# Prompt latent attention with the probabilities as the loaded operand of the values

## What is computed

```
s = (einsum("bqhn,bkhn->bhqk", qn, k_nope)
     + einsum("bqhe,bke->bhqk", qp, k_pe)) * (64 + 32) ** -0.5
mask = k_chunk[None, :] <= (pos // 64)[:, None]
p = softmax(where(mask, s, -inf), axis=-1)
return einsum("bhqk,bkhe->bqhe", p, v)      # v has 64 columns a head
```

## Time and profile before

| what | value |
|---|---|
| median of 3 runs | 3055.38 us (3051.51 to 3055.81) |
| profiled execution | 3043.57 us, span 3042.0 us |
| PE busy | 2723.2 us (90%), 17464 matmuls |
| weight loads (PEld) busy | 2505.8 us (82%) |
| DVE busy | 1467.0 us (48%) |
| ACT busy | 941.2 us (31%) |
| POOL busy | 252.0 us (8%) |
| mean granted TensorE clock | 0.939 of full speed |
| chain that ended last | PE 77%, DVE 6%, issue 6%, ACT 4% |

### The profile page before, as it was taken

How to read it: one execution, slowest core, us unless ns; L and a number is a source line. 1 busy time by engine, 2 the same in 40 slices (tenths; PEclk the granted TensorE clock), 3 DMA queues, 4 the chain that set the end, 5 groups by cost and what they waited for, 6 DMA issues and landing times.

```text
span 3042.0 us, 53054 instructions
## 1 busy us (share of the span) xinstructions
PE 2723.2 (90%) x17464; PEld 2505.8 (82%) x17464; DVE 1467.0 (48%) x2602; ACT 941.2 (31%) x2032; POOL 252.0 (8%) x684
## 2 busy tenths in 40 slices
PE   5898989789889899999988889997997999999996
PEld 5875879667689899999978568885776988999996
DVE  5635221244444674655657342213445347646375
ACT  3324223345421331322233332233453113323122
POOL 3100100110000010100001011011000001001010
PEclk8979989889999999999989899998999999999998
DMA  4220114411122222222123002234111222222222
GB/s 124 52 60 0 51 44 124 149 44 42 39 62 63 67 69 73 73 69 74 58 65 70 27 8 64 68 116 134 42 39 42 76 63 66 69 73 73 69 69 75
DMA packets 376797, 201.32 MB, mean 66 GB/s; under 512 B 66438, under 2 KB 368636, under 8 KB 376658
## 3 DMA queue, kind: packets, MB, share of 16 engines
q1 hardware_dynamic: 346722, 178.99, 21.0%
q10 hardware_dynamic: 25344, 12.27, 1.3%
q0 software_dynamic: 4592, 8.35, 0.9%
HBM read 183.84 MB, written 17.88 MB: 66 GB/s over the span
## 4 chain that ended last, share of the span: by engine, by line
PE 77%; DVE 6%; issue 6%; ACT 4%; DVEq 3%; DMA 2%; ACTq 1%; SPq 0%; POOL 0%; POOLq 0%
PE ps L547 21%; PE ps L551 20%; PE ps L548 20%; PE ps L687 1%; PE ps L644 1%; PE ps L714 1%; DVE rstd L1638 1%; DMA k_past<-in_cache_a_k 1%; ACT w_hi L1171 1%; PE ps L586 1%; PE ps L589 1%; PE ps L617 1%; PE ps L712 1%; DVEq L1749 1%; PE tp L702 1%
## 5 line engine op out<-in xcount | busy, mean ns | idle before, releaser
L547 PE MATMUL ps<-hn_hi,w_hi 128*128 128x328 f32 x2848 | 893.0, 320 | 13.7 <-DVE ob_lo L1937 7.7
L548 PE MATMUL ps<-hn_lo,w_hi 128*128 128x328 f32 x2848 | 878.3, 314 | 0.0
L551 PE MATMUL ps<-hn_hi,w_lo 128*128 128x328 f32 x2848 | 662.8, 315 | 0.0
L1620 DVE TENSOR_TENSOR w_lo<-w_raw,w_hi 128x1024 fp32r<-128x1024 f32 x300 | 366.9, 1223 | 511.4 <-ACT w_hi L1171 505.6
L1171 ACT ACTIVATE w_hi<-w_raw 128x1024 fp32r<-128x1024 f32 x300 | 316.7, 1057 | 849.0 <-PE ps L551 627.6
L547 PEld LDWEIGHTS ps<-hn_hi,w_hi 128*128 128x128 f32 x2848 | 539.1, 189 | 34.7 <-issue 29.8
L548 PEld LDWEIGHTS ps<-hn_lo,w_hi 128*128 128x128 f32 x2848 | 539.7, 190 | 0.2
L551 PEld LDWEIGHTS ps<-hn_hi,w_lo 128*128 128x128 f32 x2848 | 485.8, 189 | 0.0
L547 PE MATMUL ps<-s_hi,w_hi 128*128 128x328 f32 x704 | 220.7, 320 | 18.5 <-DVE w_lo L1620 14.0
L548 PE MATMUL ps<-s_lo,w_hi 128*128 128x328 f32 x704 | 220.3, 318 | 0.0
L551 PE MATMUL ps<-s_hi,w_lo 128*128 128x328 f32 x704 | 166.9, 320 | 0.0
(11 more groups left out here) (333 smaller groups left out, 4130.7 us busy)
## 6 DMA issues: line engine op xcount, KB each, us to landing
w_raw<-in_w_in SPq DMA_DIRECT2D x98, 512.0 KB
w_raw<-in_w_up SPq DMA_DIRECT2D x88, 512.0 KB
w_raw<-in_w_down SPq DMA_DIRECT2D x32, 512.0 KB
out<-tok_out ACTq DMA_DIRECT2D x32, 256.0 KB, 2.3
k_past<-in_cache_a_k SPq DMA_DIRECT2D x16, 512.0 KB, 5.0
v_past<-in_cache_a_v SPq DMA_DIRECT2D x16, 512.0 KB, 3.5
w_raw<-in_w_a_br SPq DMA_DIRECT2D x16, 512.0 KB
w_raw<-in_w_out SPq DMA_DIRECT2D x16, 512.0 KB
```

Of the source, the lines that this page charges most:

```text
L547: mm(dst[:, c, :], w_hi[:, slot, k, :], x_hi[:, k, cols], start=(k == 0), stop=False)
L548: mm(dst[:, c, :], w_hi[:, slot, k, :], x_lo[:, k, cols], start=False, stop=False)
L551: last = mm(dst[:, c, :], w_lo[:, slot, k, :], x_hi[:, k, cols], start=False, stop=(k == nk - 1))
L1620: tt(w_lo[:, slot], w_raw[:, slot], w_hi[:, slot].bitcast(F32), ALU.subtract).then_inc(w_split[slot], 1)
```

## The change

Four things are changed in `mla_prompt`; the rest of the kernel stays. `values` swaps its operands: the turned probabilities are loaded (128 columns) and the head's values move (64 columns), so that the output has the queries as rows. The probabilities are no longer divided: `finish` is gone, `turn` waits for "exp", and DVE's `outputs` multiplies the 128 x 64 output by the reciprocal sum while it copies it to a new buffer `o_tok` (128 queries x tile x 128, two heads side by side); the sums get four places. For each pair of heads and tile, PE turns `o_tok` once (`pair_tile`: in steps 6 and 7 of the pair and 0 and 1 of the next) into the free columns of `tq`, and DVE copies it to `obT`. The first pair is written out as well as the last, and at the end PE turns the last two tiles after a wait for all outputs, and DVE copies them.

```diff
--- before.py
+++ after.py
@@ -205,6 +205,7 @@
         d_e = (d_e0, d_e1)
         assert names["d_e0"][1] <= Z
         assert names["keyT"][0] >= names["tok_out"][1]
+        o_tok, = run(names["ckv_tok"][1], ("o_tok", [P, QT, P]))
 
         pdT2, = run(names["par_rows"][0], ("pdT2", [P, H, 2 * DEC]))
         o_sq, = run(names["par_rows"][0], ("o_sq", [P, 2, P]))
@@ -339,6 +340,10 @@
             first, last = (0, KD) if u // 2 % 2 == 0 else (0, 4)
             return [(last * (2 * (u % 2) + x) // 4, last * (2 * (u % 2) + x + 1) // 4) for x in range(2)]
 
+        def pair_tile(u, first):
+
+            return u - 6 if u >= 6 else (u + 2 if u < 2 and not first else None)
+
         OUTPUTS = STREAMS // 2 + 1
 
         block = ctx.enter_context(nc.Block())
@@ -621,7 +626,7 @@
                 def turn(i2, u):
                     i = u % QT
                     step = l * H * QT + i2 * 2 * QT + u
-                    e.wait_ge(a["p"], step + 1)
+                    e.wait_ge(a["exp"], step + 1)
                     e.wait_ge(a["pT"], step)
                     e.sem_inc(past_wait, 1)
                     p = ms[:, u % 2]
@@ -630,7 +635,7 @@
                         last = mm(tpt[0][:, 1 + k, :], p[:, META + P * k:META + P * (k + 1)], ident, is_transpose=True, start=True, stop=True)
                     last.then_inc(a["turned"], 1)
 
-                def values(i2, u):
+                def values(i2, u, first):
                     hh, i = divmod(u, QT)
                     step = l * H * QT + i2 * 2 * QT + u
                     if i == 0:
@@ -638,30 +643,39 @@
                     e.wait_ge(a["pT"], step + 1)
                     e.wait_ge(a["out_done"], step - 1 if u else step)
                     e.sem_inc(past_wait, 1)
-                    out = tq[VB * hh:VB * (hh + 1), u % 2, 0:P]
-                    mm(out, mla_vs[0:META, hh, 0, :], mla_eT[0:META, u % 2, 0, :], start=True, stop=False)
+                    tile = pair_tile(u, first)
+                    if tile is not None:
+                        mm(tq[:, u % 2, P:2 * P], o_tok[:, tile, :], ident, is_transpose=True, start=True, stop=True)
+                    out = tq[:, u % 2, 0:VB]
+                    mm(out, mla_eT[0:META, u % 2, 0, :], mla_vs[0:META, hh, 0, :], start=True, stop=False)
                     for k in range(i + 1):
-                        last = mm(out, mla_vs[:, hh, 1 + k, :], mla_eT[:, u % 2, 1 + k, :], start=False, stop=(k == i))
+                        last = mm(out, mla_eT[:, u % 2, 1 + k, :], mla_vs[:, hh, 1 + k, :], start=False, stop=(k == i))
                     last.then_inc(a["out"], 1)
 
-                def two_heads(i2, final):
+                def two_heads(i2, first, final):
                     for u in range(2 * QT):
                         then = step_after(i2, u, 2, final)
                         if then and u:
                             scores(*then)
                         if u:
-                            values(i2, u - 1)
+                            values(i2, u - 1, first)
                         turn(i2, u)
 
                     if not final:
                         scores(*step_after(i2, 2 * QT - 1, 3, final))
-                    values(i2, 2 * QT - 1)
+                    values(i2, 2 * QT - 1, first)
 
                 for u in range(3):
                     scores(0, u, first=u < 2)
-                with e.Fori(0, H // 2 - 1) as i2:
-                    two_heads(i2, False)
-                two_heads(H // 2 - 1, True)
+                two_heads(0, True, False)
+                with e.Fori(1, H // 2 - 1) as i2:
+                    two_heads(i2, False, False)
+                two_heads(H // 2 - 1, False, True)
+                e.wait_ge(a["out_done"], (l + 1) * H * QT)
+                e.sem_inc(past_wait, 1)
+                for i in range(2, QT):
+                    last = mm(tq[:, 0, (i - 1) * P:i * P], o_tok[:, i, :], ident, is_transpose=True, start=True, stop=True)
+                last.then_inc(a["p"], 1)
 
             def diff_prompt(l):
                 a = att["diff"]
@@ -1205,7 +1219,7 @@
                     e.wait_ge(a["max"], l * H * QT + i2 * 2 * QT + u + 1)
                     e.sem_inc(past_wait, 1)
                     c = 2 * (u % 2)
-                    act(ms[:, u % 2, 0:n], ms[:, u % 2, 0:n], ACT.Exp, bias=negmax[:, c:c + 1], accum_out=sums[:, c:c + 1]).then_inc(a["exp"], 1)
+                    act(ms[:, u % 2, 0:n], ms[:, u % 2, 0:n], ACT.Exp, bias=negmax[:, c:c + 1], accum_out=sums[:, u % 4:u % 4 + 1]).then_inc(a["exp"], 1)
 
                 def transposed(i2, u):
                     i = u % QT
@@ -1679,43 +1693,42 @@
                     e.drain()
                     ts(negmax[:, c:c + 1], maxes[:, c:c + 1], -1.0, None, ALU.mult).then_inc(a["max"], 1)
 
-                def finish(i2, u):
-                    n = META + P * (u % QT + 1)
-                    c = 2 * (u % 2)
-                    e.wait_ge(a["exp"], l * H * QT + i2 * 2 * QT + u + 1)
+                def outputs(i2, u, first):
+                    hh, i = divmod(u, QT)
+                    step = l * H * QT + i2 * 2 * QT + u
+                    c = u % 4
+                    e.wait_ge(a["exp"], step + 1)
                     e.sem_inc(past_wait, 1)
                     e.reciprocal(recips[:, c:c + 1], sums[:, c:c + 1])
                     e.drain()
-                    ts(ms[:, u % 2, 0:n], ms[:, u % 2, 0:n], recips[:, c:c + 1], None, ALU.mult).then_inc(a["p"], 1)
-
-                def outputs(i2, u):
-                    hh, i = divmod(u, QT)
-                    e.wait_ge(a["out"], l * H * QT + i2 * 2 * QT + u + 1)
-                    e.sem_inc(past_wait, 1)
-                    rows = slice(VB * hh, VB * (hh + 1))
-                    copy(one(obT[rows, ds(i2, 1), i * P:(i + 1) * P]), tq[rows, u % 2, 0:P]).then_inc(a["out_done"], 1)
-
-                def two_heads(i2, final):
+                    e.wait_ge(a["out"], step + 1)
+                    e.sem_inc(past_wait, 1)
+                    tile = pair_tile(u, first)
+                    if tile is not None:
+                        copy(one(obT[:, ds(i2 if u >= 6 else i2 - 1, 1), tile * P:(tile + 1) * P]), tq[:, u % 2, P:2 * P])
+                    ts(o_tok[:, i, VB * hh:VB * (hh + 1)], tq[:, u % 2, 0:VB], recips[:, c:c + 1], None, ALU.mult).then_inc(a["out_done"], 1)
+
+                def two_heads(i2, first, final):
                     for u in range(2 * QT):
-                        then = step_after(i2, u, 1, final)
-                        if then:
-                            finish(*then)
                         if u:
-                            outputs(i2, u - 1)
+                            outputs(i2, u - 1, first)
                         then = step_after(i2, u, 2, final)
                         if then:
                             maxima(*then)
                         e.drain()
-                    outputs(i2, 2 * QT - 1)
+                    outputs(i2, 2 * QT - 1, first)
 
                 for u in range(2):
                     maxima(0, u, first=True)
                 e.drain()
-                finish(0, 0)
+                two_heads(0, True, False)
+                with e.Fori(1, H // 2 - 1) as i2:
+                    two_heads(i2, False, False)
+                two_heads(H // 2 - 1, False, True)
+                e.wait_ge(a["p"], l + 1)
+                e.sem_inc(past_wait, 1)
+                copy(obT[:, H // 2 - 1, 2 * P:], tq[:, 0, P:3 * P])
                 e.drain()
-                with e.Fori(0, H // 2 - 1) as i2:
-                    two_heads(i2, False)
-                two_heads(H // 2 - 1, True)
 
             def diff_prompt(l):
                 a = att["diff"]
```

## The result

The changed kernel takes 3112.76 us (median of 4 runs, 3106.52 to 3121.66) against 3055.48 us before: 1.0195 times as long, 95% interval 1.017 to 1.022. It is slower by some 57 us; the forecast was 3105 us, 50 slower, for the reason that TensorE's clock would not come back. The profiled execution took 3106.52 us.

What follows compares the result with a forecast made beforehand. Bound: a VectorE and ScalarE chain at full clock, PE at half clock. Two stages of 122.5 us, 245 against 196.1, gave +49 us; on the median of 3055.4 that made 3105 us, range 3048 to 3130.

Steps and rivals of the forecast that it cites:

- two blocks of eight: A block is four steps (one head, tiles 0 to 3), eight a stage; two at full clock were assumed, 122.5 us a stage.
- Rival A: In the stages, the clock stays as now or better and the kernel is faster: 3048 us, 3029 at full clock throughout; chance 0.17.
- Rival B: In the values, narrow records are short (near 0.118 us), slow blocks take 14.0 us: +4 us, 3059 in all; chance 0.10.
- The block at 1.2 GHz: Four steps of one head at half clock, set by PE: 16.1 us against 15.8 before, bounds 14.0 and 18.0.
- The added turns: PE's two extra turns a block for the head pairs: 0.43 us at 1.2 GHz, 0.22 at 2.4 GHz.
- The meta product's wider load: In the values at half clock, this load is partly exposed: 0.06 us a tile, 0.24 a block.
- the time to the first values: The start of each stage, before the first values: 7 us, taken from the kernel before.
- The block at 2.4 GHz: Four steps of one head at full clock, set by PE's round trip through ScalarE: 9.84 us against 10.62, gaining 0.78.
- gaps: PE's waits between turn and values in a full-clock block, behind tile 0 filled by the widest scores: 4.27 us.
- values and meta products: PE's value records (20 x 0.117 = 2.34 us) and four meta pairs (1.44 us) in a full-clock block: 3.78 us.
- The tail: The stage's end, PE waiting for the last output, two turns, VectorE's copies: 0.8 us, between 0.3 and 1.5.

Runs made afterwards that it cites:

- absorb_after: The changed kernel, with the query absorption ahead of the stage moving 128 columns in its second product instead of 16; 3109.53 us, 1.0204 times the kernel before.
- wide: The changed kernel, with every value product moving its 64 columns twice (128 columns, second half unused); 3054.28 us, 1.0001 times the kernel before.
- fill: The changed kernel plus one unused PE product (128 rows, 256 columns moved) a step before the wait for ScalarE's copy; 3056.08 us, 1.0015 times before.
- fill_rows16: The changed kernel plus one unused PE product a step, 256 columns moved on 16 rows instead of 128; 3172.43 us, 1.0381 times the kernel before.

## Why the prediction was right

The sign, the cause and the size came out: +57 us measured, +50 forecast, within the range of 3048 to 3130. Point by point:

**The clock.** Forecast: the stages begin at 1.2 GHz as now and stay there mostly, with two blocks of eight at 2.4 GHz in each. Shown: none in layer 0 and some 2.7 in layer 1, so 2.7 in all and not 4. The number two was a choice and not worked out, and that the sum came so near is partly luck: in absorb_after, the same stage had 37.5 us at full clock in layer 0 and 2.4 in layer 1. That the narrower stream in the values is the cause is shown by wide (clock back, 58 us less, nothing else changed); the pair fill and fill_rows16 shows that idleness is not. Rival A, that less idleness keeps the clock, is out: its price of 3048 us needed as many blocks at full clock as before. The Trainium skill's page "TensorE: Matmul & The Clock Gate", section "The HAM clock gate", ties the clock to how busy PE is; here PE at 127.44 of 133.3 us busy got 0.50, and in fill_rows16 it lost the full clock after 17.10 of 17.10 us busy, so the measurements decide against that wording for products of this kind.

**The records.** Forecast 0.22 us apart at 1.2 GHz and about 0.117 at 2.4; measured 0.221 and 0.1175. Rival B (0.118 at the low clock, blocks of 14.0 us) is out. The same page of the Trainium skill, section "LDWEIGHTS (loading the stationary operand)", gives one formula for the load, by which 128 columns take 107 ns, and no clock with it. At 1.2 GHz the trace of after disagrees with it as rows 9 did, 0.221 us; at 2.4 GHz the measured 0.1175 us is near the page's figure.

**The block at 1.2 GHz.** Forecast 16.1 us; measured (15.96 + 16.46) / 2 = 16.2. That is nearer than its terms deserve. The added turns were put at 0.43 a block; against the first block, which has none (15.55), they cost 0.66. The meta product's wider load was put at 0.24 a block and costs nothing: the product takes 222.00 - 221.38 = 0.62 us, as it did in the kernel before (219.54 to 220.16). The two misses cancel. The whole stage at half clock was put at 135; layer 0 took 133.3, of which the time to the first values is 6.1 us (215.3 to 221.38) where 7 were taken over from before. So the first pair written out, which the forecast put at nothing, shows no cost there.

**The block at 2.4 GHz.** Forecast 9.84, measured 10.07, so a block gains 0.55 and not 0.78. The step that failed is one term of the sum, "The added turns of pairs: two a block, 0.22". By the lines 1766.00 and 1766.23 above, one such turn (L648) holds PE for 0.23 us, not the 0.112 of a turn in a row of turns: two take 0.46, and the missing 0.24 is that. The other terms hold (block from 1761.74): turns 1.52 against 1.57, gaps (1.00, 0.96, 1.08, 1.18) 4.22 against 4.27, values and meta products 3.84 against 3.78. As only 2.7 blocks ran so, it moved the result by under 1 us. These turns need no waited-for probabilities, yet stand behind the wait for them in PE's program, so that they come on top of the gap instead of filling it; to place them before that wait was not tried.

**The sum.** Forecast 245 us for both stages, measured 249.9. 1.3 blocks fewer at full clock cost some 8 us (6.1 each), and the shorter starts give back 1.8. The 9.2 us outside the stages, where the forecast had nothing, are within what lies between two executions, as told above. The tail was over-sized. Timelines of PE at the end of layer 0's stage, kernel before and kernel after:

```profile
311.58 0.85 PE L644 MATMUL ps<-mla_eT,mla_vs 128*64 128x128 f32 x3
...
313.69 0.66 PE L847 MATMUL tp<-consts,c_past 128*128 128x128 f32 x2 [1.25 <-issue]
```

```profile
346.00 1.97 PE L652 MATMUL ps<-mla_vs,mla_eT 128*128 128x64 f32 x8
...
349.46 0.66 PE L861 MATMUL tp<-consts,c_past 128*128 128x128 f32 x2
```

From the end of the last values to the sample stage's first turns PE lost 313.69 - 312.43 = 1.26 us before, in which it also waited, and 349.46 - 347.97 = 1.49 now: 0.2 us, under the 0.3 to 1.5 that I had bounded it by (the ends of matmuls are modelled in the profile, so the difference counts more than either figure).

## What to carry to other kernels

Before swapping the operands of a product so that fewer columns move, look at the granted clock of the stage: where it falls and comes back already, halving what moves can cost the full clock. Here a stage with a fifth less work for VectorE became a third longer in layer 0 and a fifth longer in layer 1. Don't read the clock off how busy PE looks; look at what its products move and on how many rows. Where a kernel waits on another engine in every step, a product without use in the wait can keep the clock: here 128 rows and 128 columns a step were enough, with three of 512 columns at the start (0.9942 of before), while 256 columns a step, without those at the start, ended where before stood (1.0015), with blocks of 10.6 us against 10.37. Measure it in the kernel, and against the old kernel with the same filling, since that had 0.996.

## What the runs showed of the hardware that was not expected

- Filling of 256 columns with 128 rows against the same with 16 rows: 3056.08 us against 3172.43. The slower one lost the full clock at 248.7 after PE had been busy for 17.10 of 17.10 us. That the rows count so much was not expected.
- The same products of 64 rows that move 128 columns back to back kept the full clock in five of ten absorptions (7.66 us each) and lost it in the other five; with 16 columns in every other product they lost it in all eighteen.
- Widening the stream from 64 to 128 columns costs little: 0.1175 to 0.124 us a record at full clock, 0.221 to (235.78 - 233.91) / 8 = 0.234 at half clock.
- A turn that stands alone ahead of a value product takes 0.23 us of PE at full clock (1766.00 to 1766.23 in after), in a row of turns 0.11.
